# Stick-breaking attention computed between the chunks of its query and key projection

## What is computed

```python
def stick_breaking_attention(x, w_in, w_out):
    q, k, v = jnp.split(x @ w_in, 3, axis=-1)
    ...
    for blk in range(S // Q_BLOCK):
        t0 = blk * Q_BLOCK
        L = t0 + Q_BLOCK
        z = jnp.einsum('bqhd,bkhd->bhqk', q[:, t0:L], k[:, :L]).astype(jnp.float32) * scale
        t_idx = t0 + jnp.arange(Q_BLOCK)[:, None]
        s_idx = jnp.arange(L)[None, :]
        past = s_idx < t_idx
        log_fail = jnp.where(past, jax.nn.log_sigmoid(-z), 0.0)
        later = lax.cumsum(log_fail, axis=3, reverse=True) - log_fail
        a = jnp.where(past, jnp.exp(jax.nn.log_sigmoid(z) + later), 0.0)
        outs.append(jnp.einsum('bhqk,bkhd->bqhd', a.astype(v.dtype), v[:, :L]))
    o = jnp.concatenate(outs, axis=1).reshape(B, S, N_HEADS * HEAD_DIM)
    return o @ w_out
```

## Time and profile before

| what | us |
|---|---|
| median of 3 runs | 1755.54 (1750.05 to 1757.54) |
| profiled execution | 1755.26 |
| span of its trace | 1753.5 |
| PE busy | 1665.4 (95%) |
| DVE busy | 1208.0 (69%) |
| ACT busy | 919.0 (52%) |
| value projection ends | 94.83 |
| first matmul of `stick_out` | 140.55 |

### The profile page before, as it was taken

One profiled execution on the slowest core, in us unless ns is written; L12 is line 12 of the kernel. 1 busy time (PEld: TensorE's weight loads), 2 busy tenths in 40 slices (PEclk: granted clock), 3 DMA queues, 4 the chain that ended last, 5 costly groups with the idle time before them and its releaser, 6 DMA issues.

```text
span 1753.5 us, 24897 instructions
## 1 busy us (share of the span) xinstructions
PE 1665.4 (95%) x9808; PEld 1407.4 (80%) x9808; DVE 1208.0 (69%) x1415; ACT 919.0 (52%) x1192; POOL 0.2 (0%) x4
## 2 busy tenths in 40 slices
PE   7978999999998999999998999999999989999998
PEld 5867888898886788899865768888888867789997
DVE  6956778777875777756567559777567655677754
ACT  6476664465337765567457463331233264665543
POOL 0000000000000000000000000000000000000000
PEclk9999999999999999999999999999999999999999
DMA  7813557745650466633130225446644422145552
GB/s 252 297 59 96 164 182 258 252 151 197 210 168 28 147 192 220 224 121 112 52 120 1 74 87 200 157 135 225 225 143 158 161 84 88 45 132 185 190 177 67
DMA packets 240471, 264.69 MB, mean 151 GB/s; under 512 B 7007, under 2 KB 218978, under 8 KB 240354
## 3 DMA queue, kind: packets, MB, share of 16 engines
q1 hardware_dynamic: 238428, 258.77, 45.4%
q10 hardware_dynamic: 1926, 4.32, 0.7%
HBM read 262.01 MB, written 1.05 MB: 150 GB/s over the span
## 4 chain that ended last, share of the span: by engine, by line
PE 76%; ACT 12%; DVE 8%; issue 2%; DMA 0%; ACTq 0%; DVEq 0%
PE ps L733 75%; DVE wlo L1838 2%; ACT whi L1208 2%; ACT y L1616 1%; ACT pr L1763 1%; ACT u L1619 1%; DVE y L2147 1%; PE ps L1139 1%; DVE pr L2393 1%; DVE small L2385 1%; ACT u L1404 1%; ACT y L1344 0%; ACT sbe L1720 0%; ACT sbl L1724 0%; ACT sbt L1718 0%
## 5 line engine op out<-in xcount | busy, mean ns | idle before, releaser
L733 PE MATMUL ps<-u,whi 128*128 128x512 f32 (+1 forms) x3472 | 894.3, 341 | 20.4 <-DVE u L2208 6.2
L733 PEld LDWEIGHTS ps<-u,whi 128*128 128x128 f32 x3472 | 595.6, 190 | 117.0 <-issue 16.3
L733 PE MATMUL ps<-u,wlo 128*128 128x256 f32 (+1 forms) x2116 | 647.9, 306 | 0.0
L1838 DVE TENSOR_TENSOR wlo<-raw,whi 128x2048 fp32r<-128x2048 f32 (+6 forms) x212 | 454.0, 2142 | 207.5 <-ACT whi L1208 199.7
L1208 ACT ACTIVATE whi<-raw 128x2048 fp32r<-128x2048 f32 (+6 forms) x212 | 380.7, 1796 | 217.1 <-PE ps L733 198.5
L733 PEld LDWEIGHTS ps<-u,wlo 128*128 128x128 f32 x2116 | 401.4, 190 | 19.7
L733 PE MATMUL ps<-hid,whi 128*128 128x512 f32 (+1 forms) x1212 | 353.4, 363 | 0.0
L733 PE MATMUL ps<-hid,wlo 128*128 128x256 f32 (+1 forms) x864 | 261.5, 303 | 0.0
L733 PEld LDWEIGHTS ps<-hid,whi 128*128 128x128 f32 x1212 | 216.3, 189 | 40.1 <-issue 3.4
L733 PEld LDWEIGHTS ps<-hid,wlo 128*128 128x128 f32 x864 | 163.3, 189 | 7.0
L2147 DVE SCALAR_TENSOR_TENSOR y<-idle_half,cc,y 128x1024 f32<-128x1024 f32 x70 | 89.9, 1285 | 4.9
(11 more groups left out here) (269 smaller groups left out, 1601.9 us busy)
## 6 DMA issues: line engine op xcount, KB each, us to landing
raw<-in_ffn_w_up SPq DMA_DIRECT2D x44, 1024.0 KB, 5.1
raw<-in_w_ff_in SPq DMA_DIRECT2D x32, 1024.0 KB, 5.3
raw<-in_w_ff_out SPq DMA_DIRECT2D x32, 1024.0 KB, 5.3
modw<-in_w_mod SPq DMA_DIRECT2D x112, 256.0 KB, 4.0
idle_half<-in_w_mod SPq DMA_DIRECT2D x80, 256.0 KB, 3.6
raw<-in_w_in_dil SPq DMA_DIRECT2D x18, 1024.0 KB, 5.2
raw<-in_w_in_sb SPq DMA_DIRECT2D x12, 1024.0 KB, 7.8
raw<-in_w_ple_gate SPq DMA_DIRECT2D x8, 1024.0 KB, 5.1
```

The lines of the kernel that those rows point to most:

```text
L733: return pe.matmul(out_, lhsT, rhs, start=start, stop=stop, skip_group_check=True)
L1838: nc.vector.tensor_tensor(wlo[:, s % SPLIT, 0:n], raw[:, c["r"] % RAW, 0:n], whi[:, s % SPLIT, 0:n].bitcast(F32), ALU.subtract).then_inc(* ...
```

## The change

The value projection comes first (chunks 0 to 3), then `stick_qk` (chunks 4 to 11), whose groups alternate q and k: groups 2m and 2m+1 hold q and k of heads 4m to 4m+3. From group 2 on, each group carries the attention of one pair of heads: pair j = g - 2 gets its scores after step 5 of 16, its fails after step 14, and pair g - 3 is attended right after the scores. Pairs 0 to 5 (12 heads) start there; the phase `stick` keeps pairs 6 and 7 and the attending of pair 5. The projection sums in one bank (0 or 1) instead of two, so scores have banks 2 to 5 and the attended pairs 6 and 7. It is no longer paired, and ACT evacuates it alone. ACT does in each group: the split of a later chunk, Abs, Exp, Ln of two heads, the high part of pair g - 4, two Exp, the evacuation; DVE: two masks, its split, two fails, a low part, the modulation tile. The attention's result goes to a new buffer `o2`, since `u2` is still read by the projection. Angles and conditioning now stand at the head of `stick_v`.

```diff
-                linear("stick_qk", Wi, 8, pairs(0, 2 * D), S, "qk1")
                 linear("stick_v", Wi, 8, pairs(2 * D, D, 512), S, "v", mode="V", kmax=4)
+                linear("stick_qk", Wi, 8, [(o + 256 * m, 256) for m in range(4) for o in (0, D)], S, "qk1")
                 phase("stick")
-                linear("stick_out", A["w_out_sb"][0], 8, pairs(0, D), S, "y")
+                linear("stick_out", A["w_out_sb"][0], 8, pairs(0, D), S, "y", xin=("o", 0))
...
-            if p["T"] != S or p["evac"] not in ("qk1", "y", "relu2", "gated"):
+            if p["T"] != S or p["evac"] not in ("y", "relu2", "gated"):
...
         def acc(g, T, cols=None):
+            if g["job"]["evac"] == "qk1":
+                return ps[:, g["gi"] % 2, :].rearrange("p (j c) -> p j c", j=2)
...
+            def stick_step(p, g, n):
+
+                if p["name"] == "stick_qk" and g >= 2 and n == 4:
+                    stick_scores(g - 2)
+                    if g >= 3:
+                        stick_attend(g - 3)
+                if p["name"] == "stick_qk" and g >= 2 and n == 13:
+                    stick_fails(g - 2)
...
+                    stick_scores(6)
+                    stick_attend(5)
+                    stick_scores(7)
+                    for j in (6, 7):
+                        stick_fails(j)
+                        stick_attend(j)
...
+            def stick_projections(p):
+
+                for g, grp in enumerate(p["groups"]):
+                    c = grp[0]
+                    if g >= 1:
+                        split_high(c["s"] - 1 + SPLIT)
+                    if g == 1:
+                        more_rows()
+                    mod_rows(c["r"] - 1)
+                    if g >= 2:
+                        stick_logs(2 * g - 4)
+                        stick_logs(2 * g - 3)
+                        if g >= 4:
+                            stick_high(g - 4)
+                        stick_exp(2 * g - 4)
+                        stick_exp(2 * g - 3)
+                    evac(p, grp)
...
+                    for hd in (12, 13, 14):
+                        stick_logs(hd)
+                    for hd in (12, 13, 14, 15):
+                        if hd == 13:
+                            stick_logs(15)
+                            stick_high(4)
+                        stick_exp(hd)
+                    for pair in (5, 6, 7):
+                        stick_high(pair)
...
+            def stick_projections(p):
+
+                for g, grp in enumerate(p["groups"]):
+                    c = grp[0]
+                    if g >= 3:
+                        stick_mask(2 * g - 6)
+                        stick_mask(2 * g - 5)
+                    if g >= 1:
+                        split_low(c["s"] - 1 + SPLIT)
+                    if g >= 2:
+                        stick_fail(2 * g - 4)
+                        stick_fail(2 * g - 3)
+                    if g >= 4:
+                        stick_low(g - 4)
+                    mod_keep(c["r"] - 3)
+                    mod_scaled(c["r"])
...
+                    stick_mask(10)
+                    stick_mask(11)
+                    stick_fail(12)
+                    stick_fail(13)
+                    stick_fail(14)
+                    stick_mask(12)
+                    stick_low(4)
+                    stick_fail(15)
+                    for hd in (13, 14, 15):
+                        stick_mask(hd)
+                    for pair in (5, 6, 7):
+                        stick_low(pair)
```

More of the change, by code:

```diff
@@ L535, in build @@
             at_row += n
+        stick_i = next((p["i"] for p in phases if p["kind"] == "stick"), None)
         latent_i = next((p["i"] for p in phases if p["kind"] == "cnorm"), None)
@@ L814, in _, with stick_scores @@
             swaps = [0]
+            def stick_scores(j):
+                if j == 0:
+                    for q in (0, 1):
+                        pe.wait_ge(*at("turned_copied", ("ctx", q)))
+                for hd in (2 * j, 2 * j + 1):
+                    if hd >= 4:
+                        pe.wait_ge(*at("stick_weights", (stick_i, hd - 4)))
+                if j % 2 == 0:
+                    pe.wait_ge(*at("group_read_s", ("group", phases[stick_i - 1]["groups"][j + 1][0]["gi"])))
+                for keys in range(2):
+                    for hd in (2 * j, 2 * j + 1):
+                        o, b = (hd % 2) * 64, 2 + hd % 4
+                        qh = q1[o:o + 64, j, :]
+                        if keys == 0:
+                            mm(ps[:, b, 0:256], k1[o:o + 64, j, 0:P], qh, True, False)
+                        else:
+                            mm(ps[:, b, 256:384], k1[o:o + 64, j, P:S], qh[:, P:S], False, True).then_inc(*up("scores", (stick_i, hd)))
@@ L837, in linear_pe @@
                                 steps = [(t, k) for k in range(c["kn"]) for t in tiles]
-                            for (j, c0, m), k in steps:
+                            for n, ((j, c0, m), k) in enumerate(steps):
                                 kk = c["k"] + k
@@ L1546, in mod_rows, with stick_logs, stick_exp, stick_high @@
                 nc.scalar.activation(modrow, ps[:, 7, :], ACT.Copy).then_inc(*up("mod_rows", st["i"]))
+            def stick_logs(hd):
+                b = hd % 2
+                act.wait_ge(*at("scores", (stick_i, hd)))
+                act.wait_ge(*own())
+                nc.scalar.activation(sbt[:, b, :], ps[:, 2 + hd % 4, 0:384], ACT.Abs).then_inc(*up("scalar_step"))
+                act.wait_ge(*own())
+                nc.scalar.activation(sbe[:, b, :], sbt[:, b, :], ACT.Exp, scale=-1.0).then_inc(*up("scalar_step"))
+                if hd >= 3:
+                    act.wait_ge(*at("fail_ready", (stick_i, hd - 3)))
+                act.wait_ge(*own())
+                nc.scalar.activation(sbl[:, hd % 3, :], sbe[:, b, :], ACT.Ln, bias=1.0).then_inc(*up("weights_exp", (stick_i, hd)))
+            def stick_exp(hd):
+                act.wait_ge(*at("fail_summed", (stick_i, hd)))
+                if hd >= 4:
+                    act.wait_ge(*at("attended", (stick_i, hd - 4)))
+                act.wait_ge(*own())
+                nc.scalar.activation(sba[:, hd % 4, :], ps[:, 2 + hd % 4, 0:384], ACT.Exp).then_inc(*up("stick_weights", (stick_i, hd)))
+            def stick_high(pair):
+                act.wait_ge(*at("attended", (stick_i, 2 * pair + 1)))
+                act.wait_ge(*own())
+                nc.scalar.activation(o2[:, 0, pair, :], ps[:, 6 + pair % 2, 0:S], ACT.Copy).then_inc(*up("operand_high", (stick_i, pair)))
+            def stick_projections(p):
[14 more added lines that the diff above has]
+                    evac(p, grp)
             nc.scalar.preload_act_table_set("natural_log_exp_and_others")
@@ L1626, in _ @@
                         rstd_of(p["sums"], S)
-                    for grp in p["groups"]:
+                    if p["name"] == "stick_v":
+                        angles_and_conditioning()
+                    if p["name"] == "stick_qk":
+                        stick_projections(p)
+                    for grp in p["groups"] if p["name"] != "stick_qk" else ():
                         if p["name"] == "dil_qk0" and grp[0]["g"] == 2:
@@ L2274, in _ @@
                 elif kind == "linear":
-                    for grp in p["groups"]:
+                    if p["name"] == "stick_v":
+                        conditioning()
+                    if p["name"] == "stick_qk":
+                        stick_projections(p)
+                    for grp in p["groups"] if p["name"] != "stick_qk" else ():
                         if p["mode"] == "V":
@@ L2352, in _ @@
-                    past2 = squares[:, 7:8, :].to_broadcast([P, 2, P])
-                    fail(0)
-                    fail(1)
-                    for hd in range(HEADS):
-                        if hd + 2 < HEADS:
-                            fail(hd + 2)
-                        mask(hd)
-                        if hd % 2 == 1 and hd >= 5:
-                            low(hd // 2 - 2)
-                    low(HEADS // 2 - 2)
-                    low(HEADS // 2 - 1)
+                    stick_mask(10)
```

163 lines of the change are left out of this document (60 added, 103 removed).

## The result

| | before | changed |
|---|---|---|
| median of 20 runs each, us | 1758.15 (1749.59 to 1762.54) | 1760.34 (1758.19 to 1764.46) |
| ratio, 95% interval | | 1.0023 [1.0013, 1.0033] |
| profiled execution, span | 1755.26, 1753.5 | 1760.70, 1758.9 |
| chunk 1 starts (TensorE) | 31.27 | 30.88 |
| `stick_out` starts | 140.55 | 141.80 |

The quotient of the two medians shown is 1.0012, the ratio on record 1.0023; a second set of runs of the changed kernel (e12) has 1.0018 [1.0007, 1.0030]. So the change is slower by 0.1 to 0.3%.

What follows compares the result with a forecast made beforehand. PE was taken to bound the projections, ACT the attention stage. Terms 0.6 + 20.9 + 1.5 + 17.4 = 40.4 against 45.7 us gave -5.3; with 1.7 for the clock, -3.6: forecast 1752 us, range 1745 to 1759.

Steps and rivals of the forecast that it cites:

- Start: Before chunk 1: PE still waits until 31.27 us for the second chunk's low part, so nothing moves there.
- steps of 0.359: Query/key projections: an unpaired step takes 0.359 us, 5.74 a chunk; projections +0.6 us in all.
- group of 9.35 us: Query/key groups with attention: 5.74 + 3.61 us each if nobody waits, PE bounding narrowly.
- Interleaving: Attention work in the projection: six pairs of scores and fails 16.9 us, five attendings 4.0, together +20.9.
- Rivals 2 and 4: 2: added weight loads exposed, halfway 7 us, 1759, 2%. 4: PE's gaps merely move into the projection, 1755, 16%.
- Rival 1: Groups with attention: late fails make PE wait in each; 7.5 us more, 1759.5, or 1771 at the far end; 12%.
- within 0.5% of the kernel before: Whole kernel: a change under about 8.8 us cannot be told from none; 85% chance of landing within.
- The clock, "I take 1.7, one fall less what lies in a gap": Half clock after new gaps, rest stage: 1.7 us lost, ends 0 and 3.6 (a second fall after the start gap).
- The rest stage, +17.4: Last four heads, projection's end to `stick_out`: 17.4 us, with 7 us of PE's work in it.
- The wait in group 2, +1.5: Group 2: DVE's fail ready at 68.4 us where PE wants it at 66.9, so PE waits 1.5.
- "Nothing behind `stick_out` changes; I cost them at nothing.": Behind `stick_out`: nothing changes; weight tables and fillers cost nothing, covered by PE's dense stream.
- The prediction's own test, 103 to 108 us: Stretch from 31.27 us to `stick_out`: the forecast is wrong if outside 103 to 108 us (109.3 before).

Runs made afterwards that it cites:

- e12: Changed kernel run again, untouched, for a second profile and direct comparison; 1.0018 of the kernel before.
- e1: Changed kernel with thirteen spare matmuls in the rest stage's waits, ten ahead of attending pair 6, three ahead of pair 7; 0.9988 of the kernel before.
- e5: Changed kernel with four spare matmuls in the start wait between chunks 0 and 1; 1.0013 of the kernel before.
- e3: Changed kernel with VectorE's two fails ahead of its split in group 2 alone; 1.0009 of the kernel before.
- e9: Changed kernel with sixteen one-column memsets on VectorE in groups 4 to 7; 0.9996 of the kernel before.
- e8: Changed kernel with five spare matmuls ahead of attending pair 6, none ahead of pair 7; 0.9997 of the kernel before.
- e6: Kernel before with three spare matmuls in its own start wait of 1.62 us, a control; 0.9993 of the kernel before.
- e10: The kernel of e7 with sixteen one-column memsets on VectorE added; 0.9969 of the kernel before.
- e11: The kernel of e4 with the start wait filled by spare matmuls and the sixteen VectorE memsets; 1.0000 of the kernel before.
- e15: The kernel of e10 run again, on one chip with a repeat of e7; 0.9959 of the kernel before.
- e2: Changed kernel with the rest stage reordered: all four heads' logs before exponentials, both pairs' fails before attending pair 6; 0.9978 of the kernel before.
- e7: Changed kernel with the edits of e2, e3 and e5 together; 0.9967 of the kernel before, 1750.27 us.
- e13: Kernel before with 112 one-column memsets on VectorE, eight behind each of fourteen groups, a control; 1.0009 of the kernel before.
- e4: Values first alone: projections in the changed order and form, all sixteen heads in a stage of their own as before; 1.0017 of the kernel before.

## Why the prediction missed

Steps that held:
- Start (30.88, nothing moved), steps of 0.359, added loads hidden, group of 9.35 us, no wait for `sbf` in groups 3 to 7. Interleaving costs 20.9 us of TensorE's time and no more. Rivals 2 and 4 are out. Rival 1, the fails' chain in every group, did not come either: the one late fail stays in group 2.
- That the result would lie within 0.5% of the kernel before.

Steps that failed:
- **The clock, "I take 1.7, one fall less what lies in a gap".** This is the main one. Its upper end was 3.6. Measured: 3.1 us in the rest stage (e1 against the changed profile; 2.2 to 2.5 by e12, e5 and e3), 1.5 at the head of `stick_out` (its first five steps take 3.34 us, where 1.84 stood before), and 1.7 behind group 2. I took the price of a fall from the grant of the whole stage and its likeness from the earlier trace rows, where a wait of some 2.5 us out of 3.4 was followed by a short one. The wait here was nearly twice as long, and in the five profiles that keep it at 4.3 us or more (changed, e3, e5, e9, e12) the clock was low for 10.2 to 13.7 us from within that wait to the head of `stick_out`; in none of the five was it spared. (In e3 the low clock began at 125.0, ahead of the wait, and came to 17 us in all.) The start wait, grown from 1.62 to 2.22 us, I named only for the upper end, and the wait of group 2 not at all, while each new wait is a chance for a fall: in four of eight profiles the first costs 1.7, in three of seven the second.
- **The rest stage, +17.4.** At full clock it is 18.74 (e1, e8): the attending of pair 6 starts at 12.3 us from the projection's end, not 11.5, and the last exponential and mask are 0.7 later yet. Of the first 0.8, 0.36 is VectorE's stall ahead of the mask, which no row could tell. For the rest the rows were there; I left out gaps between ten dependent steps.
- **The wait in group 2, +1.5.** Measured 1.94, VectorE's backlog, which e3 could only pass on.
- **"Nothing behind `stick_out` changes; I cost them at nothing."** True for the instructions, false for their places. Sixteen VectorE records fewer ahead move its stalls, one to a place where it lengthens a wait of TensorE to 2.75 us. In all eleven profiles with that wait a fall follows (1.9 us together in the changed profile); of the six with 2.40 or less (before, e6, e9, e10, e11, e15) two have it, e9 and e15. Another costs 0.35 near 960 us.
- The Trainium skill's "TensorE: Matmul & The Clock Gate", section "HAM oscillation — how this bites in real kernels", charges each idle gap a penalty of half the time at low clock and makes the remedy a loop without such gaps. The runs agree: 13.7 us of half clock cost 4.6 (less than half, since part of it lay in waits), and e1 and e2, which leave no long gap, take them back. I had cited the page only for the fact of a fall and then priced the shortest one.

In the sum: 109.28 - 5.3 is 104.0 without the clock. The profile's 110.92 is that plus 0.4 (group 2's wait), 1.3 (rest stage), 1.7 and 3.1 (clock), and 0.4 spread over the steps of groups 0 to 3, which I can't place further: 110.9. The prediction's own test, 103 to 108 us, failed by that sum. The two profiles differ by +5.4 us where -3.6 were forecast, 9.0 off: 5.2 in this stretch, 1.5 at the head of `stick_out`, 1.9 at 818 us and 0.35 near 960 make up 9.0; falls at other places differ too, by up to 0.7 us each, and nearly cancel. That the time still came within 0.5% of the kernel before is no merit of the mechanism: the range was wider than the whole effect. Of the 5.3 us that the change promised, 3.2 are there in this profile once the clock is left out (110.92 - 1.7 - 3.1 is 106.1, against 109.28); with e2's order of the rest stage 3.4 more come in, and e7 measures 6.4 us under the kernel before. As written, it opened two waits on TensorE (group 2, rest stage) and lengthened two (start, 818 us), and behind each of them the clock fell in some or all of the profiles.

## What to carry to other kernels

Moving work under another stage leaves a remainder, and the remainder's order is worth planning: here four heads in the order written cost 21.9 us, in a better order 15.3, and the wait of 4.3 to 4.9 us on TensorE cost its length and then 3.6 to 4.6 us more by the low clock behind it. Price each new wait of TensorE with a fall on the path behind it; if the wait can't be ordered away, try spare matmuls in it, as e1 did. And before believing a difference of 0.2% found far behind an edit, look whether a small instruction more or less on another engine moves it.

## What the runs showed of the hardware that I had not expected

- VectorE stalls for 0.36 us at instructions whose distances are multiples of 128 records of its trace (1799, 1415, 1287, 1031 from the end), with nothing in the trace that holds it; adding 16 records to the changed kernel takes all four away (e9), adding 112 to the kernel before puts them there (e13). What in the chip causes it was not tried.
- The same wait does not always bring a fall: behind 1.94 us in group 2 the clock fell in the changed kernel, e1 and e5, not in e2, e8, e9 and e12; and in e15 it fell for 3.4 us with waits of 1.1 and 0.6 us ahead of it, in e7 at the head of `stick_out` with waits of 0.9, 0.7 and 1.1. One profile shows one draw; the mean granted clock over all timed executions (49 and 47 against 37 us of half clock, 34 in e1) was the steadier witness, but not of everything: e4 has 35 and is slower than the kernel before.
